# Latent projections as three-product splits, differential scores two heads at a time, and other homes for high parts, in a hybrid-attention and mixture-of-experts layer

## What is computed

```
proj = rms_norm(h) @ w_in                # 768 q latents, 256 kv latents, 32 k_pe, dq, dk, dv (512 each), 2 x 1024 gates
q  = rms_norm(q_lat) @ w_uq              # 768 -> 8 heads x 96
kv = rms_norm(kv_lat) @ w_ukv            # 256 -> 8 heads x (64 + 64)
o_a = causal attention of 8 heads (q, k normed, last 32 of 96 rotated)
o_b = causal attention of 8 half heads (q, k normed, all 64 rotated), in pairs: o[0] - lambda * o[1], normed
h = h + (sigmoid(gate_a) * (o_a @ w_branch_mla) + sigmoid(gate_b) * (o_b @ w_branch_diff)) @ w_out
h = h + sum over 32 experts of gate * (swiglu(t @ w1[e] + b1[e]) @ w2[e] + b2[e]),  t = rms_norm(h), top 4
```

## Time and profile before

| | us |
|---|---|
| median of 3 executions | 1143.38 (1142.67 to 1143.54) |
| the profiled execution | 1143.16 |
| its span, first to last instruction | 1141.3 |
| PE busy in the span | 1081.6 (95%) |
| DVE busy | 324.4 (28%) |
| ACT busy | 188.7 (17%) |
| mean DMA rate | 384 GB/s |
| granted TensorE clock | 1.000 |

### The profile page before, as it was taken

One profiled execution on the slowest core, in us unless ns is written; L12 is line 12 of the kernel. 1 busy time (PEld: TensorE's weight loads), 2 busy tenths in 40 slices (PEclk: granted clock), 3 DMA queues, 4 the chain that ended last, 5 costly groups with the idle time before them and its releaser, 6 DMA issues.

```text
span 1141.3 us, 12783 instructions
## 1 busy us (share of the span) xinstructions
PE 1081.6 (95%) x5152; PEld 500.1 (44%) x5152; DVE 324.4 (28%) x582; ACT 188.7 (17%) x324; POOL 36.7 (3%) x45
## 2 busy tenths in 40 slices
PE   8999999999999999999999898989898989898987
PEld 8867788744343434334343333333242424242422
DVE  4666766522221212122122112112121212120202
ACT  6646566410000000000000000000000000000000
POOL 1005320000000000000000000000000000000000
PEclk9999999999999999999999999999999999999999
DMA  9754239799999999999999999999999999999997
GB/s 368 276 185 142 80 112 356 307 431 426 427 430 413 427 428 428 427 427 428 427 430 428 428 428 428 428 428 428 430 428 429 429 428 429 428 428 428 426 425 295
DMA packets 35044, 438.66 MB, mean 384 GB/s; under 512 B 4032, under 2 KB 4288, under 8 KB 7104
## 3 DMA queue, kind: packets, MB, share of 16 engines
q1 hardware_dynamic: 34128, 431.46, 90.4%
q10 hardware_dynamic: 880, 6.69, 1.5%
HBM read 437.08 MB, written 1.05 MB: 384 GB/s over the span
## 4 chain that ended last, share of the span: by engine, by line
PE 69%; DMA 28%; ACT 1%; DVE 1%; issue 1%; SPq 0%; ACTq 0%; DVEq 0%
PE bank L825 19%; PE bank L798 18%; DMA ring<-in_expert_w 16%; PE bank L430 12%; DMA pool_r<-in_expert_w 11%; PE bank L771 5%; PE bank L739 5%; PE bank L413 3%; PE bank L717 2%; PE bank L482 1%; PE bank L518 1%; DMA acc_r<-in_x 1%; PE bank L493 1%; PE bank L769 0%; PE bank L543 0%
## 5 line engine op out<-in xcount | busy, mean ns | idle before, releaser
L798 PE MATMUL bank<-ring,feat_r 128*64 128x512 f32 x1488 | 332.0, 596 | 28.5 <-DMA ring<-in_expert_w 28.5
L798 PEld LDWEIGHTS bank<-ring,feat_r 128*64 128x64 f32 x1488 | 102.4, 137 | 249.2 <-issue 194.8
L825 PE MATMUL bank<-ring,feat_r 128*64 128x512 f32 x768 | 172.1, 596 | 7.5 <-DMA ring<-in_expert_w 7.1
L1477 DVE TENSOR_SCALAR gate_r<-bank 128x512 f32<-128x512 f32 x32 | 22.1, 692 | 439.3 <-PE bank L798 439.3
L430 PE MATMUL bank<-ring_s,feat_s 128*128 128x512 f32 (+2 forms) x448 | 136.1, 386 | 1.1 <-DVE ring_s L1205 0.9
L798 PE MATMUL bank<-pool_r,feat_r 128*64 128x512 f32 x512 | 116.3, 597 | 4.9 <-DMA pool_r<-in_expert_w 4.9
L825 PEld LDWEIGHTS bank<-ring,feat_r 128*64 128x64 f32 x768 | 53.5, 137 | 113.1 <-issue 108.0
L1151 ACT ACTIVATE gate_r<-gate_r 128x512 f32<-128x512 f32 x32 | 20.2, 630 | 480.4 <-DVE gate_r L1477 480.4
L1501 DVE TENSOR_TENSOR acc_r<-bank,acc_r 128x512 f32<-128x512 f32 x64 | 44.3, 692 | 151.7 <-PE bank L771 151.7
L430 PEld LDWEIGHTS bank<-ring_s,feat_s 128*128 128x128 f32 x448 | 80.1, 188 | 16.5 <-issue 3.4
L430 PE MATMUL bank<-ring_s 128*128 128x512 f32 (+2 forms) x224 | 84.3, 377 | 0.0
(11 more groups left out here) (193 smaller groups left out, 623.4 us busy)
## 6 DMA issues: line engine op xcount, KB each, us to landing
ring<-in_expert_w SPq DMA_DIRECT2D x138, 2048.0 KB, 32.1
pool_r<-in_expert_w SPq DMA_DIRECT2D x47, 2048.0 KB, 31.4
ring<-in_head_w SPq DMA_DIRECT2D x23, 1024.0 KB, 5.0
ring<-in_head_w SPq DMA_DIRECT2D x7, 768.0 KB, 9.9
ring<-in_expert_w SPq DMA_DIRECT2D x5, 1024.0 KB, 33.4
qkT_r<-in_expert_w ACTq DMA_DIRECT2D x1, 2048.0 KB, 12.4
late_r<-in_expert_w ACTq DMA_DIRECT2D x1, 2048.0 KB, 33.0
gate_r<-in_expert_w ACTq DMA_DIRECT2D x1, 2048.0 KB, 13.4
```

What stands on the lines that cost most here:

```text
L798: mm = pe.matmul(b[e * SLOTS:(e + 1) * SLOTS, :], xT[:, k, e * SLOTS:(e + 1) * SLOTS], w[:, e, g, :], start=(late and k == 0), stop=(k == ...
L825: mm = pe.matmul(bank[4 + h][e * SLOTS:(e + 1) * SLOTS, :], aT[k // 4][:, k % 4, e * SLOTS:(e + 1) * SLOTS], w[:, q, e, :], start=(k == 0) ...
L1477: ts(glu[:, f], bank[2 * f][:], LIMIT, None, ALU.min).then_inc(sem(f"glu_ready{f}"), 1)
```

## The change

- w_uq and w_ukv are split like the other chunks (`chunk_hi`, `up_lo`), and so are the turned latents: the high part `latT[0]` in the space of `pool_r` as before, the low part `latT[1]` in the second half of the gates' space, by four subtractions on DVE (`latT_lo`). PE makes three products for each of the 32 plain ones (`up_part`).
- Sums of squares, norm and rotation of dq and dk are done apart (`qkd_square`, `qkd_root`, `qkd_sum`, `qkd_rotate`), dq's while PE is at dk, and the low parts of chunks 10 to 13 stand between them on DVE. The high parts of chunks 14 to 17 move to later places of ACT's program.
- The scores of differential heads 2i and 2i + 1 are issued together (`diff_scores`): the two heads' operands lie in partitions 0 to 63 and 64 to 127, and their matmuls alternate.
- In the step of differential head 7 the first half of the gate product stands behind the transposes of head 6, and the second half goes into the step after. The 32 transposes that follow wait for less, each for the bank that it writes.
- The head's chunks get other homes (`HEAD_HOMES`, `HI_HOMES`), and the high part of chunk 30 goes into `merged`'s space, once `merged` has been turned. High parts rotate over three slots by the chunk's own number; chunk 31's takes the slot of chunk 29's. The experts' places 2 to 7 are then loaded at `ring_used` of 26, 28, 29, 30, 32, 32 (`FREE_AT`).
- The squares of qka get a space for each block, and the squares of h go to `spare`.

```diff
+HEAD_HOMES, HI_HOMES = (0, 1, 2, 3, 6, 7, 8, 9), (4, 5, 10)
+FREE_AT = NHEAD - 6, NHEAD - 4, NHEAD - 3, NHEAD - 2, NHEAD, NHEAD
-        latT = v3(latT_r, KQ + KKV)
+        latT = v3(pool_s[:], KQ + KKV), v3(gate_s[:, NM * D:], KQ + KKV)
+            if n == NHEAD - 2:
+                return tok_s[:, 0:nk * cols], lo
+            hi = HI_HOMES[(n if n < NHEAD - 2 else n - 2) % BUFFERS] * SLOT
-                        sp.wait_ge(ring_used, min(NHEAD - HEAD_RING + 2 * (place - EXTRA + 1), NHEAD))
+                        sp.wait_ge(ring_used, FREE_AT[place - EXTRA])
...
+            pe.wait_ge(sem("latT_ready"), 4)
+            def up_part(b, n, k, first, m, c, at, ends):
+                hi, lo = (v3(v, HEAD[n][2]) for v in split_views(n))
+                for left, right in ((0, hi), (0, lo), (1, hi)):
+                    mm = pe.matmul(b, latT[left][:, k, m * P:(m + 1) * P], right[:, at, c], ...)
+            for i, n in enumerate(UP[:-1]):
+                pe.wait_ge(sem("up_ready"), i + 1)
...
+            pe.wait_ge(sem("up_ready"), len(UP))
...
+            def diff_scores(i):
+                if i:
+                    pe.wait_ge(sem("scored"), 2 * i)
+                for m in range(NM):
+                    for a in range(2):
+                        half = slice(a * DD, (a + 1) * DD)
+                        mm = pe.matmul(bank[a][:, m * P:(2 * m + 1) * P], dqkT[half, i, m * P:(m + 1) * P],
+                                       dqkT[half, SUB // 2 + i, 0:(m + 1) * P], ...)
...
-                    if s > 0:
+                    if s >= SUB:
                         scores(s)
+                    elif s > 0 and s % 2 == 0:
+                        diff_scores(s // 2)
-                    gate_part(s, 0)
+                    if s != SUB - 1:
+                        gate_part(s, 0)
                 if s > first:
                     probs_turn(s - 1)
-                if s < last:
+                if s == SUB - 1:
+                    gate_part(s, 0)
+                elif s < last:
                     gate_part(s, 1)
+                elif s == SUB:
+                    gate_part(s - 1, 1)
...
+            def chunk_hi(n, halves=1):
                 act.wait_ge(head_landed[n % HEAD_RING], 16 * (n // HEAD_RING + 1))
-                if i >= BUFFERS:
-                    act.wait_ge(ring_used, SPLIT[i - BUFFERS] + 1)
+                if n == NHEAD - 2:
+                    act.wait_ge(sem("merged_turned"), 2 * NM)
+                elif n >= BUFFERS:
+                    act.wait_ge(ring_used, (n if n < NHEAD - 2 else n - 2 + BUFFERS) - BUFFERS + 1)
...
+            split_lo(9)
+            for m in range(NM):
+                qkd_sum(0, m)
+            for m in range(NM):
+                for i in range(2):
+                    latT_lo(m, i)
+            qkd_rotate(0, 0)
+            up_lo(0)
+            qkd_rotate(0, 1)
+            up_lo(1)
+            up_lo(2)
+            for m in range(NM):
+                qkd_sum(1, m)
+            qkd_rotate(1, 0)
+            up_lo(3)
+            qkd_rotate(1, 1)
+            for i in range(10, 13):
                 split_lo(i)
```

More of the change, by code:

```diff
@@ L102, in lap_of @@
     return 1 if n - NHEAD in ONCE else ring_place(n) // WIDE + 1
+UP = [n for n, c in enumerate(HEAD) if c[0] in ("w_uq", "w_ukv")]
 HEAD_AT = [P * sum(nk * cols for _, _, nk, _, cols in HEAD[:n]) for n in range(NHEAD)]
@@ L162, in build @@
         qkaT = v3(qkT_r[:], 2 * HA)
-        squares = qkT_r[:, 0:2 * HA * QK_A]
+        squares = [qkT_r[:, m * 2 * HA * QK_A:(m + 1) * 2 * HA * QK_A] for m in range(NM)]
         o_b = qkd_r[:, 0:NM * WD].rearrange("p (m h d) -> p m h d", m=NM, h=HD)
@@ L473, in _ @@
             pe.wait_ge(sem("unit_copied"), 2 * 6)
-            n0 = chunk_index("w_uq", 0, 0)
+            pe.wait_ge(sem("latT_ready"), 4)
             HQ = HA * QK_A // 2
-            for i in range(KQ // 2):
-                arrive(n0 + i)
-                w = head_view(n0 + i)
+            def up_part(b, n, k, first, m, c, at, ends):
+                hi, lo = (v3(v, HEAD[n][2]) for v in split_views(n))
+                for left, right in ((0, hi), (0, lo), (1, hi)):
+                    mm = pe.matmul(b, latT[left][:, k, m * P:(m + 1) * P], right[:, at, c],
+                                   start=(first and left == 0 and right is hi), stop=(ends and left == 1),
+                                   skip_group_check=True)
+                return mm
+            for i, n in enumerate(UP[:-1]):
+                pe.wait_ge(sem("up_ready"), i + 1)
                 for h, b in enumerate(bq):
@@ L481, in _ @@
                         for k in (2 * i, 2 * i + 1):
-                            mm = pe.matmul(b[m][:, 0:HQ], latT[:, k, m * P:(m + 1) * P], w[:, k - 2 * i, h * HQ:(h + 1) * HQ],
-                                           start=(k == 0), stop=(k == KQ - 1), skip_group_check=True)
+                            mm = up_part(b[m][:, 0:HQ], n, k, k == 0, m, slice(h * HQ, (h + 1) * HQ), k - 2 * i, k == KQ - 1)
                 mm.then_inc(ring_used, 1)
-            n0 = chunk_index("w_ukv", 0, 0)
-            arrive(n0)
-            w = head_view(n0)
+            pe.wait_ge(sem("up_ready"), len(UP))
             for h in range(2):
@@ L1057, in _ @@
                         probsT_copy(s - 1)
+                    if s == SUB and not lo:
+                        gates_copy(s - 1)
                     if s >= SUB + HA - 1 and lo:
@@ L1242, in _, with up_lo, latT_lo @@
                     .then_inc(sem("lat_ready"), 1)
-            for i in range(9, 12):
+            def up_lo(i):
+                n = UP[i]
+                _, _, nk, _, cols = HEAD[n]
+                hi, lo = split_views(n)
+                dve.wait_ge(sem("hi_ready"), n + 1)
+                tt(lo, head_slot(n, nk * cols), hi, ALU.subtract).then_inc(sem("up_ready"), 1)
+            def latT_lo(m, i):
+                dve.wait_ge(sem("unit_copied"), 9 + 2 * m + i)
+                c = slice(m * P, (m + 1) * P)
+                tt(latT[1][:, 4 * i:4 * i + 4, c], v3(bank[2 * m + i][:], 4), latT[0][:, 4 * i:4 * i + 4, c],
+                   ALU.subtract).then_inc(sem("latT_ready"), 1)
@@ new lines, in qkd_sum, with qkd_rotate @@
+            def qkd_sum(h, m):
+                dve.wait_ge(sem("qkd_squared"), 2 * h + m + 1)
+                dve.tensor_reduce(ssq[:, 8 + 16 * m + 8 * h:16 + 16 * m + 8 * h],
+                                  v3(tok_r[:, (2 * h + m) * WD:(2 * h + m + 1) * WD], SUB), AX.X, ALU.add)\
+                   .then_inc(sem("qkd_summed"), 1)
+            def qkd_rotate(h, m):
+                i = 2 * h + m
+                qk = qkd[:, m, h * SUB:(h + 1) * SUB]
+                r = slice(8 + 16 * m + 8 * h, 16 + 16 * m + 8 * h)
+                dve.wait_ge(sem("qkd_rooted"), i + 1)
+                link(dve.reciprocal(rstd[:, r], ssq[:, r]))
+                link(tt(qk, qk, rstd[:, r].unsqueeze(2).broadcast_to([P, SUB, DD]), ALU.mult))
+                link(tt(qk, qk, g_qkd[:, h * DD:(h + 1) * DD].unsqueeze(1).broadcast_to([P, SUB, DD]), ALU.mult))
+                half = DD // 2
+                x1, x2 = qk[:, :, 0:half], qk[:, :, half:]
+                cos, sin = (tab_v[:, m, ROPE_A + o:ROPE_A + o + half].unsqueeze(1).broadcast_to([P, SUB, half])
+                            for o in (0, half))
+                a, b, c, d = (v3(gate_r[:, o * SUB * half:(o + 1) * SUB * half], SUB) for o in range(4))
+                for dst, x_, by in ((a, x1, cos), (b, x2, sin), (c, x2, cos), (d, x1, sin)):
+                    tt(dst, x_, by, ALU.mult).then_inc(sem("qkd_rotated"), 1)
+                dve.wait_ge(sem("qkd_rotated"), 4 * i + 4)
+                tt(x1, a, b, ALU.subtract).then_inc(sem("qkd_ready"), 1)
+                tt(x2, c, d, ALU.add).then_inc(sem("qkd_ready"), 1)
@@ L1257, in _ @@
-            split_lo(12)
-            for m in range(NM):
                 dve.wait_ge(sem("qka_squared"), m + 1)
-                dve.tensor_reduce(ssq[:, 8 + 16 * m:24 + 16 * m], v3(squares, 2 * HA), AX.X, ALU.add)\
+                dve.tensor_reduce(ssq[:, 8 + 16 * m:24 + 16 * m], v3(squares[m], 2 * HA), AX.X, ALU.add)\
                    .then_inc(sem("qka_summed"), 1)
```

121 lines of the change are left out of this document (61 added, 60 removed).

## The result

The changed kernel takes 1137.77 us (median of five, 1137.23 to 1138.53); the kernel before, beside it, 1143.38 (five, 1142.67 to 1144.04). The ratio is 0.995 with a 95% interval of 0.9939 to 0.9961: 5.6 us faster, where 5.0 was forecast. The profiled execution took 1137.9 us, with a span of 1135.5 at a granted clock of 1.000.

A forecast was written before the change was run, and what follows sets the result against it. The end was taken to follow PE's start on the experts, since DMA waits for PE near 350 us. Terms -3.6 - 2.3 - 1.0 + 1.9 = -5.0 us gave 1138.4 us, range 1133.5 to 1141.2.

The forecast's parts named there:

- The bound: Whole kernel: the end moves one to one with the time at which PE begins the experts.
- Rival (b): DMA stream: filling the 5 to 7 us hole at 220 us gains as much again, 1132 to 1134; 0.15 with all-good ends.
- The latents: w_uq and w_ukv in three products on PE: -3.6 us, between -4.4 and -2.4, including small waits for DVE.
- Scores by twos: Differential heads' scores issued in pairs that overlap on PE: -2.3 us, between -0.6 and -2.6.
- a head's price: Differential scores: one head's four records take 0.85 us, and a pair of heads was taken to cost the same.
- PSUM Bottleneck: Differential scores, rival (a): evacuation eats the gain, leaving 0.6 to 1.0 us, 1139.7 to 1140.1; chance 0.2.
- The last differential step: Head 7's step: -1.0 us, between 0 and -2.3, with a new 1.6 us wait for ACT's copy.
- Chunk 31: End of the head: its cast waits for chunk 29's slot, so PE waits; +1.9 us, between +1.5 and +2.2.
- The loads: Experts' places 4 and 5 load earlier and fill the hole at 220 us: no gain.
- the share was to be full from 215 to 225 us: Sign of being right: a full DMA share in that stretch, the earlier loads filling the hole.
- The longer dip near 345 us: Sign of being right: the DMA engines idle longer there, waiting for PE, after earlier loads in the head.
- The sum: All terms together: -3.6 - 2.3 - 1.0 + 1.9 = -5.0 us, giving 1138.4 us.

The follow-up runs named there:

- e1: Changed kernel with the experts' places 4 and 5 released as before the change, at 30 and 32 chunks used; 1137.88 us.
- e4: Changed kernel with 40 useless transposes added on PE ahead of the first scores; 1141.88 us.
- e2: Changed kernel with chunk 31's high part in chunk 28's slot and the experts' places 4 to 7 released only at 32 chunks used; 1139.09 us.
- e5: Changed kernel with w_uq and w_ukv multiplied as plain 32-bit floats again, without split parts; dq and dk still normed apart; 1141.38 us.
- e6: Changed kernel with the differential scores issued one head at a time, as before the change; 1140.78 us.
- e7: Changed kernel with head 7's gate product, and its copy on ACT, back in their old place; relaxed bank waits kept; 1137.08 us.
- e3: Changed kernel with high parts' slots rotating 4, 10, 5, chunk 31's following chunk 28's, and places 4 and 5 both released at 30 chunks used; 1135.40 us.
- e9: Changed kernel without the two low-part products for w_uq and w_ukv on PE, the parts still made (output lacks them); 1137.07 us.
- e10: Changed kernel with the edits of e3 and e8 joined; 1135.00 us.
- e12: e10 with eight useless transposes put into two of PE's waits between the router's matmuls; 1134.46 us.
- e8: Changed kernel with ACT copying head 6's turned probabilities ahead of head 7's exponentials instead of behind them; 1136.85 us.

## Why the prediction was right

**The bound.** It held. In thirteen of fourteen kernels the experts take 896.1 to 896.7 us from PE's first product on, although their starts lie 8.7 us apart. e1 shows that earlier loads bring nothing, e4 that a delay of PE early in the head costs nearly its whole length. Rival (b), that the hole in the DMA stream counts, is refuted where a dip is left (its 5 to 7 us would have given 1131.4 to 1133.4, not the 1132 to 1134 that the prediction has), and e2 shows the point from which it would be true: without a dip, a chunk loaded late costs 3.8 us of its 4.9.

**The latents, -3.6.** Measured -3.59 at the transposes and -3.6 in e5. The parts moved against each other: the waits for DVE were 0.28 us ahead of chunk 13 and next to nothing ahead of chunk 11, in place of 0.8 together, and the work was some 0.5 longer than 17.9. DVE's chain, worked out operation by operation from rows of other shapes, ended within half a microsecond of the forecast: chunk 13 was there at 70.8, forecast 70.9. ACT's copies ahead of the scores stayed hidden, as forecast: they end at 83.26 and PE starts the scores at 83.70.

**Scores by twos, -2.3.** Measured -2.7 (1.07, 0.81 and 0.81 for the three pairs), and -3.0 for the whole edit in e6, the fourth pair's share in the last step included. The overlap was taken rightly. The mis-sized term is a head's price: 0.85 is the time from its own first record to the next matmul, but the matmul before it was also 0.09 longer (0.32 from its start to that of the scores, 0.23 between others), so a head not issued saves 0.94. Beside it, PE waits 0.13 us in an odd step for ACT's copy, as charged (0.1).
The Trainium skill's rule, TensorEngine Tiling (Array Packing), Performance Considerations, PSUM Bottleneck, is right in kind, since ACT's copy is what PE then waits for; but it took 0.13 us a step here and not the gain. The Trainium skill, TensorEngine Tiling (Array Packing), Key Properties, says that a change of tiling mode drains the engine. The 0.09 us agrees with that; no run here separates a drain from another cause.

**The last differential step, -1.0.** Measured -1.1, with a wait of 1.36 for ACT's copy where 1.6 was forecast. The prediction's own times give 133.05 - 131.9 = 1.15, which it wrote down as 1.0. The number was right, but it hid that the part as edited holds a loss: of what changes in this step, the move of the gate product costs 0.5 (e7), so that the scores and the relaxed waits bring 1.6 together, by difference. The forecast saw the new wait and did not ask what the old order would have made of it.

**Chunk 31, +1.9.** The wait is 1.73 us in PE's record; the lead falls by 7.53 - 5.68 = 1.85 there, and by 2.1 to the experts' start when e3 takes the cause away. Also right: it was the price of loads that bring nothing.

**The loads, 0.** Right, but one sign was wrong: the share was to be full from 215 to 225 us. Two loads went out at 198.57 and 204.12 and were done by about 216, and the next waited for the head's last chunk at 219.44. The hole was moved, not filled. The longer dip near 345 us came as forecast, but the forecast lacks the dips at 230 and 245 us, in which more of the gain was idled away (e1). That the loads are worth nothing holds all the same.

**The sum.** -3.63 up to the first scores, -2.68 up to step 6, -0.10 in step 6, -1.12 in step 7, then +1.85 at chunk 31 and +0.18 from there to the experts: -5.50. The span is 5.8 shorter, 0.3 of it in the tail, within what executions of one kernel differ by.

What stays open: why the clock fell in the profiled executions of e4, e6, e9 and e10 just ahead of the experts and in no other, although PE's waits there are the same, and how often it does so in executions that were not profiled.

## What to carry to other kernels

Where DMA engines and PE take turns as the bound, find the last place at which the transfers wait for the computation: up to there each microsecond of the computation counts wholly and bytes loaded earlier count nothing, until that dip is used up. Compare marks, not totals: the distance between two marks that no edit touches (here 896.2 us) tells at once whether a difference arose ahead of them. Where an edit adds a wait and still wins, split it; here one of three moves gave back 0.5 us, and a slot that was chosen for earlier loads 1.9.

## What the runs showed of the hardware

- **The second half-height product at once was free here.** The eight records of two heads' scores (K = 64, alternating between partitions 0 to 63 and 64 to 127) take 0.93 us; the four of one head on one half take 0.92 (e6).
- **The clock ahead of the experts.** In the router's stretch the lowest granted clock of 5 us was 0.74, 0.66, 0.69 and 0.74 in e4, e6, e9 and e10, and 1.00 in the other ten kernels. The waits of 0.64 and 0.38 us in that stretch are the same in all of them but e12, so they alone don't decide it. In e10 the same records took 1.19 against 0.68 us. It costs up to about a microsecond, as much as some of the edits, so a comparison of marks behind that stretch needs its clock beside it.
- **The clock in the latents of e9** was 0.66, 0.83 and 0.50 in the stretches from 60 to 75 us, in which PE waited 2.62 and 4.48 us: here work taken from an engine that waits for another was partly lost to its clock.
- **Where DMA was the bound a lower clock cost nothing that shows.** In the stretch from 1050 to 1055 us it was 0.72 in e7 and 0.76 in e8, and the experts took 896.3 us all the same.
